# Splitting the weights of the routing's early expert projections, and four more of them in the routing

## The chip, the core and the metric

The kernel runs on one core of one Trainium2 chip. The metric is the device time of one execution in microseconds, the median of the runs shown; less is better. TensorE does the matmuls, ScalarE (ACT) and VectorE (DVE) the elementwise work, GpSimd (POOL) elementwise work in SBUF, and SyncE (SP) issues the DMAs.

## The reference, cut to what matters

Two transformer blocks run over 256 tokens of width 1024. The first ends in a product-key expert layer, and the change lies there:

```python
def chunk_fn(xc):
    q = (xc @ w_query).reshape(C, PEER_HEADS, 2, PEER_HALF)
    sc = jnp.einsum('thpd,hpnd->thpn', q, sub_keys)
    top_s, top_i = lax.top_k(sc, PEER_TOPK)
    cand_s = (top_s[:, :, 0, :, None] + top_s[:, :, 1, None, :]).reshape(...)
    best_s, best_pos = lax.top_k(cand_s, PEER_TOPK)
    gates = jax.nn.softmax(best_s, axis=-1)
    u = expert_down[experts]
    vv = expert_up[experts]
    act = jax.nn.gelu(jnp.einsum('cd,chkd->chk', xc, u), approximate=False)
    return jnp.einsum('chk,chkd->cd', gates * act, vv)
```

## The kernel before

All 16,384 experts are computed for all tokens and weighted with a mostly empty matrix of gates. They are cut into 128 chunks of 128 experts. Each chunk needs a projection (eight k-steps of a 128x128 block of `expert_down` against the 256 tokens), a Gelu, a multiplication with the gates and a product with `expert_up`.

Four stages follow each other, and a block of all engines ends each of the first three.

1. `route_phase`. Sixteen rounds make the query projections and key scores. TensorE's matmuls feed VectorE, which finds the top 16 of each (`top16`). VectorE then works alone: for eight heads it adds two lists into `cand` (L1545) and searches them, and it then forms the index of each chosen expert in four rounds of `match` (L1568), `picked` (L1571) and a reduction (L1575). Meanwhile TensorE does the projections of the first `EARLY` = 24 chunks (`Ahead.project`, L1300), as plain float32 matmuls on the loaded weights `raw`, and ScalarE the Gelus (L1311). The gates' exponential (L1514) stands behind the Gelu of chunk `BEFORE_GATE` - 1. At the end TensorE waits for VectorE's indices and gates and turns them (L1489). SP loads a half chunk as soon as TensorE has read the half that lies in its buffer (L1292).
2. `spread_phase` builds the matrix of gates from one-hot products, 32 groups of eight tokens, and between them TensorE does `LATE` = 20 more plain projections. `early` holds the first `READY` = `EARLY` + `LATE` chunks, already multiplied with their gates; `spread` holds the gates of the others.
3. `experts_phase`. For the first `READY` chunks TensorE only adds (12 matmuls of 512 columns, `add`). For the others it does `both`: the projection of the next chunk in three passes (`Projections`), and the addition.
4. The second block of the reference.

A projection in three passes has both operands split into a float32r part and the rest. ScalarE copies the weight to `high`, another engine subtracts it from the raw weight to give `low`, and TensorE makes `high`x`high`, `high`x`low` and `low`x`high` (L230, L231, L232). The query projections of the routing are split in this way already, in buffers `w_high` and `w_low`: ScalarE at L1499, GpSimd at L1450, half a chunk (128x512) each time. In the expert stage VectorE makes `low`.

The order of each engine's work is the program's order; engines meet at semaphores. `over_chunks` writes chunks 0 and 1 out and loops over pairs behind them.

Of the kernel before, what the change touches and what calls it, by code (L numbers as in the profile page):

```python
# [22 lines left out]
F32 = mybir.dt.float32  # L23
# [3 lines left out]
ALU = mybir.AluOpType  # L27
ACT = mybir.ActivationFunctionType
# [3 lines left out]
SEQ = 256  # L32
NT = SEQ // P
D = 1024
KD = D // P
# [6 lines left out]
HEADS_P = 8  # L42
TOPK = 16
SLOTS = HEADS_P * TOPK
EARLY = 24
LATE = 20
BEFORE_GATE = 16
LEAD = 8
FINE = 8
READY = EARLY + LATE  # L50
REST = 1
# [107 lines left out]
def wait(eng, sem, value):  # L159

    if isinstance(value, int) and value <= 0:
        return
    eng.wait_ge(sem, value)
# [51 lines left out]
def second_row_high(act, hT, full, ready):  # L215

    for n in (2, 3):
        act.activation(row_window(hT[0], n), row_window(full, n), ACT.Copy).then_inc(ready, 1)
# [9 lines left out]
def three_passes(pe, out, lhs, rhs, start, stop):  # L228

    pe.matmul(out, lhs[0], rhs[0], start=start, stop=False, skip_group_check=True)  # L230
    pe.matmul(out, lhs[0], rhs[1], start=False, stop=False, skip_group_check=True)  # L231
    return pe.matmul(out, lhs[1], rhs[0], start=False, stop=stop, skip_group_check=True)  # L232
# [1081 lines left out]
class Projections:  # L1314
# [18 lines left out]
    def half(self, h):  # L1333
        return slice(KD // 2 * h, KD // 2 * (h + 1))
# [33 lines left out]
def over_chunks(eng, lo, hi, one):  # L1368

    if lo == 0:  # L1370
        one(0, 0)
        one(1, 1)
        lo = 2
    with eng.Fori(lo // 2, hi // 2) as i:
        for b in range(2):
            one(i * 2 + b, b)


def route_phase(nc, weights, hT, whole, sbt, slots, raw, landed, early, ahead):
# [3 lines left out]
    HP = 2 * HEADS_P  # L1383
    NW = len(raw)
    with ExitStack() as c:  # L1385
        def sb(n, s, dt=F32):
            return c.enter_context(nc.sbuf_tensor(f"route_{n}", s, dt))
# [4 lines left out]
        def sem(n):  # L1392
            return c.enter_context(nc.semaphore(f"route_{n}"))
# [11 lines left out]
        shifted = sb("shifted", [P, NT, SLOTS])  # L1405
        gate = sb("gate", [P, NT, SLOTS])
# [8 lines left out]
        w_high, w_low = [[sb(f"{n}{b}", [P, KD, P], F32R) for b in range(2)] for n in ("w_high", "w_low")]  # L1415
        q_ready, q_kept, s_ready, s_kept, w_highs, w_lows = [sem(n) for n in ("q", "q_kept", "s", "s_kept", "w_highs", "w_lows")]
        shifted_ready, gate_exp, cols_ready = [sem(n) for n in ("shifted", "gate_exp", "cols")]
        row_high, row_low = sem("row_high"), sem("row_low")
        block = c.enter_context(nc.Block())

        def steps(eng, one):
            rounds = HP // NW
            for b in range(NW):
                one(b, b, 0)
            with eng.Fori(1, rounds - 1) as i:
                for b in range(NW):
                    one(i * NW + b, b, i)
            for b in range(NW):
                one((rounds - 1) * NW + b, b, rounds - 1)

        @block.sync
        def _(sp):

            for b in range(2):
                ahead.load(sp, b, b)
            with sp.Fori(0, HP // NW - 1) as i:
                for b in range(NW):
                    sp.wait_ge(s_ready, i * NW + b + 1)
                    sp.dma_start(raw[b][:], weights[i * NW + b + NW]).then_inc(landed[b], 16)
            over_chunks(sp, 2, EARLY + 2, lambda n, b: ahead.load(sp, n, b))  # L1440

        @block.gpsimd
        def _(pool):
            def weight_low(hp, b, i):
                if isinstance(hp, int) and hp < 2:
                    return
                for h in range(2):
                    k = slice(KD // 2 * h, KD // 2 * (h + 1))
                    pool.wait_ge(w_highs, hp * 2 + (h - 3))
                    pool.tensor_tensor(w_low[b % 2][:, k], raw[b][:, k], w_high[b % 2][:, k].bitcast(F32),  # L1450
                                       ALU.subtract).then_inc(w_lows, 1)
            steps(pool, weight_low)

        @block.tensor
        def _(pe):
            def one(hp, b, i):
                wait(pe, q_kept, hp - 1)
                first = isinstance(hp, int) and hp < 2
                if isinstance(hp, int) and hp == 2:
                    pe.wait_ge(row_low, 2)  # L1460
                for k in range(KD):
                    if first:
                        mm = pe.matmul(ahead.u[b][:, P:SEQ], raw[b][:, k, :], ahead.h[:, k, P:SEQ], start=k == 0, stop=k == KD - 1,
                                       skip_group_check=True)
                        continue
                    if k % (KD // 2) == 0:
                        pe.wait_ge(w_lows, hp * 2 + (k // (KD // 2) - 3))
                    mm = three_passes(pe, qp[b % 2][:, 0:SEQ], [v[b % 2][:, k, :] for v in (w_high, w_low)],
                                      [v[:, k, :] for v in hT], k == 0, k == KD - 1)
                mm.then_inc(q_ready, 1)  # L1470
                if not isinstance(hp, int) or hp > 0:
                    scores_of(hp - 1, (b - 1) % NW)

            def scores_of(hp, b):
                pe.wait_ge(q_kept, hp + 1)
                if isinstance(hp, int) and hp < 2:
                    pe.wait_ge(landed[b], 16)
                wait(pe, s_kept, hp - 1)
                for t in range(NT):
                    mm = pe.matmul(sp_[b % 2][:, t * P:(t + 1) * P], qh[b % 2][:, t * P:(t + 1) * P], raw[b][:, KD, :],  # L1480
                                   start=True, stop=True)
                mm.then_inc(s_ready, 1)
            steps(pe, one)
            scores_of(HP - 1, NW - 1)
            over_chunks(pe, 0, EARLY, lambda n, b: ahead.project(pe, n, b))
            for n, src in enumerate((index[1], coarse, fine, gate)):
                pe.wait_ge(cols_ready, n + 1)
                for t in range(NT):
                    pe.transpose(slots[:, n, t * P:(t + 1) * P], src[:, t, :], sbt["ident"][:])  # L1489

        @block.scalar
        def _(act):
            def weight_high(hp, b, i):
                act.wait_ge(landed[b], i * 16 + 16)
                if not isinstance(hp, int) or hp > 3:
                    wait(act, q_ready, hp - 1)
                for h in range(2):
                    k = slice(KD // 2 * h, KD // 2 * (h + 1))
                    act.activation(w_high[b % 2][:, k], raw[b][:, k], ACT.Copy).then_inc(w_highs, 1)  # L1499

            def one(hp, b, i):
                if not isinstance(hp, int) or 2 <= hp + 1 < HP:
                    weight_high(hp + 1, (b + 1) % NW, i + (b + 1) // NW)
                act.wait_ge(q_ready, hp + 1)
                wait(act, s_ready, hp - 1)
                steps_in = ahead.u[b] if isinstance(hp, int) and hp < 2 else qp[b % 2]
                act.activation(qh[b % 2][:], steps_in[:, 0:SEQ], ACT.Copy).then_inc(q_kept, 1)
            second_row_high(act, hT, whole, row_high)
            steps(act, one)
            def early_chunk(n, b):  # L1510
                ahead.gelu(act, n, b, early[:, n, :])
            over_chunks(act, 0, BEFORE_GATE, early_chunk)
            act.wait_ge(shifted_ready, 1)
            act.activation(gate[:], shifted[:], ACT.Exp).then_inc(gate_exp, 1)  # L1514
            over_chunks(act, BEFORE_GATE, EARLY, early_chunk)

        @block.vector
        def _(dve):
# [80 lines left out]
def spread_phase(nc, slots, iota, early, spread, ahead, load_first):  # L1599
# [15 lines left out]
    def merged_rows(g):  # L1615

        return EARLY + sum(j <= g for j in joins)

    with ExitStack() as c:
# [13 lines left out]
        @block.sync  # L1633
        def _(sp):
            for n in range(EARLY + 2, READY):
                ahead.load(sp, n, n % 2)
            sp.wait_ge(ahead.projected, READY * 2)
            load_first(sp)
# [437 lines left out]
```

## Time and profile before

| | |
|---|---|
| median of 3 runs | 1578.44 us (1575.54 to 1579.21) |
| profiled execution | 1575.72 us, its span 1573.9 us |
| busy: TensorE, VectorE, ScalarE, GpSimd | 98%, 64%, 44%, 3% of the span |
| projections in the routing | 234.5 to 317.5 us |
| spread stage | 318 to 448 us |
| expert stage | 449 to 1044 us |

A share of busy time says how full an engine is, not how much of its work could go. The time of the profiled execution is 1.8 us above its span; sums are made against it.

### The profile page before, as it was taken

The page shows a single profiled execution, that of the slowest core. Times are in us where ns is not written, and L with a number is a line of the kernel's source. Part 1 is how long each engine was busy: PE and PEld are TensorE (multiplying, and loading weights), DVE is VectorE, ACT ScalarE, POOL GpSimd, SP SyncE. Part 2 cuts the span into 40 slices and gives each one's busy share as a digit, 9 for nine tenths or more (in the row PEclk, how much of TensorE's full clock was granted, in tenths as well). Part 3 has the DMA queues.
Part 4 walks back from the last instruction along what each step waited for, and adds up shares of the span by engine and source line. Part 5 has one row for each costly group of instructions (what it writes and reads, how often), then busy time and mean ns, then how long its engine had stood idle before and what let it go on. Part 6 is the DMA issues. An engine that isn't in the chain of part 4 may idle for free. (4 is left out here: it accounts for less than half of the span.)

```text
span 1573.9 us, 29022 instructions
## 1 busy us (share of the span) xinstructions
PE 1535.9 (98%) x8999; PEld 1339.9 (85%) x8999; DVE 1008.4 (64%) x2440; ACT 692.3 (44%) x1478; POOL 41.9 (3%) x42
## 2 busy tenths in 40 slices
PE   7998999999999999999999999999999999999998
PEld 4665798889978889999999999979999999759994
DVE  4666589978877766666666666665555555247762
ACT  2443241222234444444444444446666666326651
POOL 0000260000000000000000000000000000000000
PEclk9999999999999999999999999999999999999999
DMA  7420244422245555555555555557544444317630
GB/s 289 160 101 1 70 139 148 153 94 86 82 160 188 196 189 188 186 187 186 187 187 187 187 186 187 186 172 228 176 148 148 147 147 147 94 39 224 172 101 27
DMA packets 163511, 239.30 MB, mean 152 GB/s; under 512 B 41712, under 2 KB 91376, under 8 KB 161904
## 3 DMA queue, kind: packets, MB, share of 16 engines
q1 hardware_dynamic: 163440, 238.42, 46.6%
q8 instruction: 37, 0.61, 0.1%
q14 instruction: 34, 0.28, 0.1%
HBM read 237.09 MB, written 1.29 MB: 151 GB/s over the span
## 5 line engine op out<-in xcount | busy, mean ns | idle before, releaser
L230 PE MATMUL experts_acc<-experts_uh,experts_wh 128*128 128x512 f32 x512 | 200.6, 392 | 1.6 <-DVE experts_ul L1838 1.6
L231 PE MATMUL experts_acc<-experts_ul,experts_wh 128*128 128x512 f32 x512 | 200.2, 391 | 0.0
L232 PE MATMUL experts_acc<-experts_uh,experts_wl 128*128 128x512 f32 x512 | 199.2, 389 | 0.0
L232 PE MATMUL projection<-hT_high,down_low 128*128 128x256 f32 x672 | 190.2, 283 | 0.0
L231 PE MATMUL projection<-hT_low,down_high 128*128 128x256 f32 x672 | 190.1, 283 | 0.0
L230 PE MATMUL projection<-hT_high,down_high 128*128 128x256 f32 x672 | 189.7, 282 | 0.0
L1808 ACT ACTIVATE experts_uh<-whole 128x512 fp32r<-128x512 f32 x256 | 146.8, 624 | 67.2 <-PE experts_acc L232 60.9
L1838 DVE TENSOR_TENSOR experts_ul<-whole,experts_uh 128x512 fp32r<-128x512 f32 x256 | 164.8, 685 | 1.9 <-ACT experts_uh L1808 1.9
L1300 PE MATMUL plain_u<-whole,down_raw 128*128 128x256 f32 x704 | 157.3, 379 | 0.4 <-PEq L1385 0.4
L1300 PEld LDWEIGHTS plain_u<-whole,down_raw 128*128 128x128 f32 x704 | 131.3, 190 | 17.2 <-issue 0.7
L1844 DVE TENSOR_TENSOR experts_full<-experts_full,spread 128x256 f32<-128x256 f32 x84 | 35.8, 426 | 158.1 <-ACT experts_full L1365 158.1
L231 PEld LDWEIGHTS projection<-hT_low,down_high 128*128 128x128 f32 x672 | 128.7, 191 | 3.2
L230 PEld LDWEIGHTS projection<-hT_high,down_high 128*128 128x128 f32 x672 | 128.7, 191 | 3.2
L230 PE MATMUL mix_a_pj<-mix_a_wh,hT_high 128*128 128x384 f32 x368 | 129.1, 351 | 0.0
L232 PEld LDWEIGHTS projection<-hT_high,down_low 128*128 128x128 f32 x672 | 128.7, 191 | 0.0
L1341 ACT ACTIVATE down_high<-down_raw 128x512 fp32r<-128x512 f32 x168 | 105.2, 632 | 43.5 <-DMA down_raw<-in_downT 42.8
L232 PE MATMUL mix_a_pj<-mix_a_wh,hT_low 128*128 128x384 f32 x368 | 123.5, 336 | 0.0
L231 PE MATMUL mix_a_pj<-mix_a_wl,hT_high 128*128 128x384 f32 x368 | 123.5, 336 | 0.0
L1365 ACT ACTIVATE experts_full<-projection 128x256 f32<-128x256 f32 x84 | 32.3, 384 | 205.5 <-PE projection L232 205.5
L232 PEld LDWEIGHTS experts_acc<-experts_uh,experts_wl 128*128 128x128 f32 x512 | 96.2, 188 | 20.7
L230 PEld LDWEIGHTS experts_acc<-experts_uh,experts_wh 128*128 128x128 f32 x512 | 96.5, 188 | 20.3 <-DVE experts_ul L1838 1.0
L231 PEld LDWEIGHTS experts_acc<-experts_ul,experts_wh 128*128 128x128 f32 x512 | 96.5, 188 | 16.7
(392 smaller groups left out, 3001.5 us busy)
## 6 DMA issues: line engine op xcount, KB each, us to landing
down_raw<-in_downT SPq DMA_DIRECT2D x256, 256.0 KB, 3.5
whole<-in_up SPq DMA_DIRECT2D x256, 256.0 KB, 2.8
mix_raw<-in_wa SPq DMA_DIRECT2D x46, 768.0 KB, 6.1
block_w_raw<-in_w SPq DMA_DIRECT2D x16, 768.0 KB, 6.1
mix_raw<-in_wb SPq DMA_DIRECT2D x16, 768.0 KB, 6.7
route_raw<-in_route SPq DMA_DIRECT2D x16, 576.0 KB, 3.8
wo<-in_wo SPq DMA_DIRECT2D x4, 1024.0 KB, 8.2
mix_a_w_gate<-in_wa SPq DMA_DIRECT2D x8, 512.0 KB, 7.3
```

The source lines that it names most:

```text
L230: pe.matmul(out, lhs[0], rhs[0], start=start, stop=False, skip_group_check=True)
L231: pe.matmul(out, lhs[0], rhs[1], start=False, stop=False, skip_group_check=True)
L232: return pe.matmul(out, lhs[1], rhs[0], start=False, stop=stop, skip_group_check=True)
L1300: mm = pe.matmul(self.u[b][:, 0:SEQ], self.raw[b][:, k, :], self.h[:, k, :], start=k == 0, stop=k == KD - 1, skip_group_check=True)
L1341: act.activation(self.high[b][:, self.half(h)], self.raw[b][:, self.half(h)], ACT.Copy).then_inc(self.highs, 1)
L1365: act.activation(into, self.u[b][:, 0:SEQ], ACT.Gelu).then_inc(self.done, 1)
L1808: act.activation(uh[b][:, w], raw_u[b][:, w], ACT.Copy).then_inc(u_high, 1)
L1838: dve.tensor_tensor(ul[b][:, w], raw_u[b][:, w], uh[b][:, w].bitcast(F32), ALU.subtract).then_inc(u_low, 1)
L1844: dve.tensor_tensor(full[:], full[:], spread[:, n - READY, :], ALU.mult)
```

## The change

`EARLY` goes from 24 to 28, so `READY` goes from 44 to 48, and `BEFORE_GATE` from 16 to 22. Chunks 0 and 1 stay plain. Chunks 2 to 27 of the routing are projected in three passes: ScalarE makes `w_high`, GpSimd `w_low`, TensorE 24 matmuls in place of 8. SP reloads a raw half when GpSimd has subtracted from it, where before it waited for TensorE. ScalarE makes the `high` of chunk n+1 before the Gelu of chunk n. The buffers `w_high` and `w_low` are those of the query projections.

```diff
@@ -42,9 +42,10 @@
 HEADS_P = 8
 TOPK = 16
 SLOTS = HEADS_P * TOPK
-EARLY = 24
+EARLY = 28
+SPLIT = 28
 LATE = 20
-BEFORE_GATE = 16
+BEFORE_GATE = 22
 LEAD = 8
 FINE = 8
 READY = EARLY + LATE
@@ -1418,6 +1419,15 @@
         row_high, row_low = sem("row_high"), sem("row_low")
         block = c.enter_context(nc.Block())
 
+        QUERY_HALVES = (HP - 2) * 2
+
+        def halves_split(n, h):
+
+            return QUERY_HALVES + (n - 2) * 2 + h + 1
+
+        def half(h):
+            return slice(KD // 2 * h, KD // 2 * (h + 1))
+
         def steps(eng, one):
             rounds = HP // NW
             for b in range(NW):
@@ -1437,7 +1447,16 @@
                 for b in range(NW):
                     sp.wait_ge(s_ready, i * NW + b + 1)
                     sp.dma_start(raw[b][:], weights[i * NW + b + NW]).then_inc(landed[b], 16)
-            over_chunks(sp, 2, EARLY + 2, lambda n, b: ahead.load(sp, n, b))
+
+            def load_split(n, b):
+                for h in range(2):
+                    sp.wait_ge(w_lows, halves_split(n - 2, h))
+                    sp.dma_start(ahead.raw[b][:, half(h)], ahead.down[n][:, half(h)]).then_inc(ahead.landed[b][h], 16)
+            for b in range(2):
+                ahead.load(sp, 2 + b, b)
+            over_chunks(sp, 4, SPLIT + 2, load_split)
+            if SPLIT < EARLY:
+                over_chunks(sp, SPLIT + 2, EARLY + 2, lambda n, b: ahead.load(sp, n, b))
 
         @block.gpsimd
         def _(pool):
@@ -1450,6 +1469,13 @@
                     pool.tensor_tensor(w_low[b % 2][:, k], raw[b][:, k], w_high[b % 2][:, k].bitcast(F32),
                                        ALU.subtract).then_inc(w_lows, 1)
             steps(pool, weight_low)
+
+            def down_low(n, b):
+                for h in range(2):
+                    pool.wait_ge(w_highs, halves_split(n, h))
+                    pool.tensor_tensor(w_low[b][:, half(h)], ahead.raw[b][:, half(h)], w_high[b][:, half(h)].bitcast(F32),
+                                       ALU.subtract).then_inc(w_lows, 1)
+            over_chunks(pool, 2, SPLIT, down_low)
 
         @block.tensor
         def _(pe):
@@ -1482,7 +1508,21 @@
                 mm.then_inc(s_ready, 1)
             steps(pe, one)
             scores_of(HP - 1, NW - 1)
-            over_chunks(pe, 0, EARLY, lambda n, b: ahead.project(pe, n, b))
+
+            def project_split(n, b):
+                for h in range(2):
+                    pe.wait_ge(w_lows, halves_split(n, h))
+                    if h == 0:
+                        pe.wait_ge(ahead.done, n - 1)
+                    for k in range(KD // 2 * h, KD // 2 * (h + 1)):
+                        mm = three_passes(pe, ahead.u[b][:, 0:SEQ], [v[b][:, k, :] for v in (w_high, w_low)],
+                                          [v[:, k, :] for v in hT], k == 0, k == KD - 1)
+                    mm.then_inc(ahead.projected, 1)
+            for b in range(2):
+                ahead.project(pe, b, b)
+            over_chunks(pe, 2, SPLIT, project_split)
+            if SPLIT < EARLY:
+                over_chunks(pe, SPLIT, EARLY, lambda n, b: ahead.project(pe, n, b))
             for n, src in enumerate((index[1], coarse, fine, gate)):
                 pe.wait_ge(cols_ready, n + 1)
                 for t in range(NT):
@@ -1507,12 +1547,36 @@
                 act.activation(qh[b % 2][:], steps_in[:, 0:SEQ], ACT.Copy).then_inc(q_kept, 1)
             second_row_high(act, hT, whole, row_high)
             steps(act, one)
-            def early_chunk(n, b):
+
+            def down_high(n, b):
+                for h in range(2):
+                    act.wait_ge(ahead.landed[b][h], (n - b) * 8 + 16)
+                    act.wait_ge(ahead.projected, n * 2 + (h - 3))
+                    act.activation(w_high[b][:, half(h)], ahead.raw[b][:, half(h)], ACT.Copy).then_inc(w_highs, 1)
+
+            def plain_chunk(n, b):
                 ahead.gelu(act, n, b, early[:, n, :])
-            over_chunks(act, 0, BEFORE_GATE, early_chunk)
-            act.wait_ge(shifted_ready, 1)
-            act.activation(gate[:], shifted[:], ACT.Exp).then_inc(gate_exp, 1)
-            over_chunks(act, BEFORE_GATE, EARLY, early_chunk)
+
+            def split_chunk(n, b):
+                down_high(n + 1, 1 - b)
+                plain_chunk(n, b)
+
+            def gates():
+                act.wait_ge(shifted_ready, 1)
+                act.activation(gate[:], shifted[:], ACT.Exp).then_inc(gate_exp, 1)
+            plain_chunk(0, 0)
+            split_chunk(1, 1)
+            first = min(BEFORE_GATE, SPLIT - 2)
+            over_chunks(act, 2, first, split_chunk)
+            if BEFORE_GATE < SPLIT:
+                gates()
+                over_chunks(act, first, SPLIT - 2, split_chunk)
+            split_chunk(SPLIT - 2, 0)
+            plain_chunk(SPLIT - 1, 1)
+            if BEFORE_GATE > SPLIT:
+                over_chunks(act, SPLIT, BEFORE_GATE, plain_chunk)
+                gates()
+                over_chunks(act, BEFORE_GATE, EARLY, plain_chunk)
 
         @block.vector
         def _(dve):
```

## Rows read from the trace of the kernel before

**Rows 1.** The page: busy time by engine, granted TensorE clock in 40 slices.

```profile
PE 1535.9 (98%) x8999; PEld 1339.9 (85%) x8999; DVE 1008.4 (64%) x2440; ACT 692.3 (44%) x1478; POOL 41.9 (3%) x42
...
PEclk9999999999999999999999999999999999999999
```

**Rows 2.** Busy time by stretch: length, PE, PEld, DVE, ACT, POOL, clock, DMA.

```profile
290.00:318.00 28.00, 28.00 (x134) 24.67 (x133) 24.31 (x21) 10.23 (x15) 0.00 (x0) 1.00 0.47 152
330.00:446.00 116.00, 115.76 (x763) 106.94 (x762) 94.85 (x128) 31.93 (x97) 0.00 (x0) 1.00 0.24 78
```

**Rows 3.** ScalarE in order of time, projections of the routing.

```profile
238.16 0.38 ACT L1311 ACTIVATE early<-plain_u 128x256 f32<-128x256 f32 x1 [2.96 <-PE plain_u L1300]
...
290.45 1.28 ACT L1514 ACT_TABLE_LOAD   x1
...
300.48 1.28 ACT L1311 ACT_TABLE_LOAD   x1 [3.14 <-PE plain_u L1300]
...
317.68 0.38 ACT L1311 ACTIVATE early<-plain_u 128x256 f32 x1 [1.72 <-PE plain_u L1300]
```

**Rows 4.** All engines in order of time, where the routing ends.

```profile
315.12 0.49 DVE L1595 TENSOR_TENSOR route_gate<-route_gate,route_ginv 128x128 f32<-128x128 f32 x2
...
317.39 0.38 PE L1489 MATMUL slots<-ident,route_index 128*128 128x128 f32 x2
```

**Rows 5.** TensorE in order of time, one round of the routing.

```profile
193.75 0.36 PE L230 MATMUL route_qp<-hT_high,route_w_high 128*128 128x256 f32 x1
...
196.71 0.61 PE L1480 MATMUL route_sp<-route_raw,route_qh 128*128 128x128 f32 x4
197.07 0.36 PE L230 MATMUL route_qp<-hT_high,route_w_high 128*128 128x256 f32 x1
```

**Rows 6.** Tiles projection and experts_acc: ns min/median/max, first and last start.

```profile
L230 PE MATMUL projection<-hT_high,down_high x672: 277/283/283, 571.2 to 1037.4; 128*128 128x256 f32 x168
...
L230 PE MATMUL experts_acc<-experts_uh,experts_wh x512: 389/389/504, 450.4 to 1043.2; 128*128 128x512 f32 x171
...
L232 PE MATMUL experts_acc<-experts_uh,experts_wl x512: 387/389/397, 451.0 to 1043.6; 128*128 128x512 f32 x171
```

**Rows 7.** GpSimd in order of time: its first pieces and a late round.

```profile
185.73 5.00 POOL L1450 TENSOR_TENSOR route_w_low<-route_raw,route_w_high 128x512 fp32r<-128x512 f32 x4 [169.28 <-ACT route_w_high L1499]
...
228.96 2.53 POOL L1450 TENSOR_TENSOR route_w_low<-route_raw,route_w_high 128x512 fp32r<-128x512 f32 x2 [1.32 <-ACT route_w_high L1499]
```

**Rows 8.** VectorE in order of time, four places of the routing.

```profile
183.34 1.30 DVE L225 TENSOR_TENSOR hT_low<-whole,hT_high 128x512 fp32r<-128x512 f32 x2 [1.39 <-ACT hT_high L218]
...
240.46 0.75 DVE L1545 TENSOR_TENSOR route_cand<-route_topv 128x256 f32<-128x256 f32 x2
...
282.34 0.49 DVE L1555 TENSOR_TENSOR route_shifted<-route_bestv 128x128 f32<-128x128 f32 x2
...
283.65 2.29 DVE L1568 TENSOR_TENSOR route_match<-route_partf,iota 128x2048 f32<-128x2048 f32 x1
```

**Rows 9.** VectorE's groups by shape, 240.4 to 317 us.

```profile
L1571 DVE TENSOR_TENSOR route_picked<-route_match,route_topi 128x2048 f32<-128x2048 f32 x4 | 9.2, 2292 | 0.3
...
L1575 DVE TENSOR_REDUCE route_index<-route_picked 128x128 f32<-128x2048 f32 x4 | 9.1, 2286 | 0.3
...
L1545 DVE TENSOR_TENSOR route_cand<-route_topv 128x256 f32<-128x256 f32 x16 | 6.1, 422 | 0.5
```

**Rows 10.** Tiles route_w_low and route_rest: ns min/median/max, first and last start.

```profile
L1450 POOL TENSOR_TENSOR route_w_low<-route_raw,route_w_high x28: 1266/1286/1297, 185.7 to 230.2; 128x512 fp32r<-128x512 f32 x28
...
L1526 DVE MAX8 route_topv<-route_rest x32: 276/286/297, 188.8 to 239.1; 128x8 f32<-128x128 f32 x32
```

**Rows 11.** ScalarE's groups by shape, 180 to 460 us.

```profile
L1499 ACT ACTIVATE route_w_high<-route_raw 128x512 fp32r<-128x512 f32 x28 | 16.2, 625 | 7.7 <-DMA route_raw<-in_route 7.7
```

**Rows 12.** Tile down_raw, 234 to 318 us: from issue to landing.

```profile
DMA to landing us min/median/max: 2.5/2.7/3.0
```

**Rows 13.** VectorE's groups, 318 to 449 us.

```profile
L1670 DVE TENSOR_TENSOR early<-early,spread_g 128x208 f32<-128x208 f32 (+20 forms) x32 | 14.0, 436 | 21.6 <-ACT spread L1722 21.6
```

## The prediction, made before the change was run

> **What bounds the kernel now.** I read the page first: TensorE is busy 98% of the span, at the full clock (2.4 GHz) in every slice [rows 1]. Then the table by stretch, for the end of the routing and the spread stage: TensorE is busy throughout, and VectorE nearly so [rows 2]. Then the order of time where the routing ends. TensorE sets it, but only just: VectorE's last gate operation ends at 315.6 (315.12 + 0.49), and TensorE starts to turn its results at 317.39, as soon as the last projection is through [rows 4]. So VectorE's chain of top-16 searches and index arithmetic has 1.8 us of slack; whatever takes more than that from the projections' time only uncovers it. Last, I looked for who else works there: GpSimd does nothing behind 231.5 (its last piece starts at 228.96), and its pieces before that are the same subtraction that the change adds [rows 7].
>
> **The terms on TensorE.** A plain projection: the Gelus follow each other from 238.16 to 317.68, 23 intervals, 3.457 us each [rows 3]; 24 take 83.0. A projection in three passes: in the routing its 24 matmuls and the step to the scores take 2.96 us (193.75 to 196.71) [rows 5]. In the expert stage 44 additions alone take 450.4 to 571.2, 2.745 each, and 84 of projection and addition 571.2 to 1043.6, 5.624 each, which leaves 2.88 for the projection [rows 6]. I take 2.88.
>
> - Expert stage: four chunks fewer need a projection there: 4 x 2.88 = -11.5 us. Their Gelus, splits and loads go too, but they lie beside TensorE. This term I hold for sure.
> - Routing: 2 x 3.457 + 26 x 2.88 = 81.8 in place of 83.0, -1.2 us, if TensorE is never made to wait.
> - Spread stage: VectorE's merge covers four rows more, 32 elements of some 1.05 ns (2048 elements take 2.29 us and 256 take 0.42 [rows 9]) x 32 groups = 1.1 us, and it idles 21.6 us there [rows 13]. TensorE is busy 115.76 of 116 us [rows 2] with unchanged work. Nothing.
>
> **Supply.** A chunk needs from ScalarE two copies of 0.6 us [rows 11] and a Gelu of 0.38 [rows 3], from GpSimd two halves, 2.53 us [rows 7], of 2.88. GpSimd is thus 88% full. The loop through ScalarE, with an estimated 0.1 at each handover: end of chunk n-1, Gelu 0.38, first copy 0.6, first subtraction 1.28, three handovers: 2.6 of the 2.88 that TensorE spends on chunk n. The loop through SP: a load lands in 2.7 us [rows 12], then 0.6 + 1.28 and three handovers make 4.9 of the 5.76 that a buffer has. Both close, with little to spare. At the start, chunks 2 and 3 cannot be loaded before chunk 0 and 1 are read: about +0.5 us. The exponential of the gates now stands before the copy of chunk 23: load of its table 1.28, itself 0.42, so the loop takes 4.3 in place of 2.6 once, +1.4 us; and the Gelu's table is loaded again in the loop every second chunk behind it (300.48, as now [rows 3]), 3.9 in place of 2.6, +1.0. These 2.9 us count only if nothing slower covers them. VectorE's own use of the gates comes at 314, and the indices are ready for the exponential at 283 [rows 8], chunk 21's end is about 299: no wait for VectorE.
>
> **The unknown: GpSimd beside VectorE.** Until now GpSimd worked only beside VectorE's searches, which read one operand. Next to those neither is slowed: a subtraction takes 1266 to 1297 ns in all 28 cases, a MAX8 276 to 297 with and without GpSimd [rows 10]. But VectorE's operations on two operands in SBUF never met it: the last before GpSimd ends at 184.64 (183.34 + 1.30) and GpSimd starts at 185.73 [rows 7, 8]. Now 26 x 2.53 = 66 us of subtraction run beside 16 `cand` additions (6.1 us) and eight operations of 2.29 us (18.3 us) on two operands [rows 9]. The cost lies between nothing and full exclusion, where one waits until the other is done. Rows that lean to the upper end: GpSimd takes 1286 ns for 512 elements of two operands where ScalarE takes 625 for 512 of one [rows 10, 11], as if operands were fetched one after the other on a path that is scarce. And with GpSimd 88% full, a loss of over 12% reaches TensorE whole. I take the upper end. Its price, with each waiting its turn:
>
> - Heads, 240.46 to 282.34 [rows 8]: GpSimd is busy 88% of the time, so an addition waits 0.88 x 0.64 = 0.56 us on average, 16 of them 9 us: VectorE's index stage starts at 283.65 + 9 = 292.6. GpSimd loses 0.75 us per head, about its slack, so TensorE goes on at 2.9 per chunk from 241.9 and has done 19.5 chunks by then.
> - Four index rounds: `match` 2.29, one half subtraction 1.28, `picked` 2.29, two halves 2.53 beside the reduction of 2.29 = 8.4 us for three halves, one chunk and a half. 4 x 8.4 = 33.6 us, to 326.2, 25.5 chunks. TensorE gets a chunk per 5.6 us here and idles half the time.
> - VectorE's path is free then: 2.5 x 2.88 = 7.2, end at 333.4. If GpSimd gets both halves between `match` and `picked`, the rounds are longer and more chunks are done in them; the end is the same within 1 us, since it is a sum of turns. VectorE's chain ends near 329.
> - Two additions of 0.42 take 0.75 together [rows 8]: starts overlap. Over some 48 changes of turn I take off 1.5 us: 332.
>
> The Trainium skill speaks against this change here. "SBUF — State Buffer", section "Who interferes with whom", says that a VectorE instruction with two SBUF inputs and a GpSimd instruction that reads SBUF take one shared read port in turn, the second blocking for the whole length of the first. No row before shows it; by it the sum is the upper end, without it the first rival below.
>
> **Sum of the forecast.** Routing's projections end at 332 in place of 317.5: +14.5. Experts -11.5. Together +3.0: 1575.7 becomes 1578.7 profiled. The median stands 2.7 above the profiled execution, so 1581.4, say 1581. If a start-up part of 0.15 us (0.42 less 256 x 1.05 ns) holds no path, the end is 330 or a little less; with more lost at each turn 337: own range 1575 to 1587.
>
> **Rivals.**
>
> 1. *No contention.* For it: the unslowed rows above [rows 10]. The projections end at 234.5 + 81.8 + 2.9 = 319.2, past VectorE's 315.6: +1.7 - 11.5 = -9.8, 1568.6 us. Chance 0.33.
> 2. *VectorE is starved, slower.* If GpSimd, with its next half already queued, goes first whenever both ask, an addition waits 1.9 us in place of 0.56. The heads take 16 x 1.9 = 30 more and end near 314, GpSimd is done near 318, and the 29 us of index rounds then stand alone, to 346. From the point that VectorE's waits sum to over 16 us (332 - 315.6) it sets the end. +29 - 11.5 = +17, 1596 us. Against it: GpSimd has a gap in each round [rows 7]. Chance 0.04.
> 3. *The clock falls.* TensorE is busy 2.88 of 5.6 us in the index rounds; if the granted clock, 2.4 GHz now, goes to 1.2, a chunk costs 5.76, and the last 2.5 chunks 7.2 more, then a few us of the spread stage: 1591 us. No row before has so loose a stretch. Chance 0.03.
> 4. *Partial sharing*, between forecast and first rival, about 1575: 0.06.
>
> **Numbers.** Forecast 0.54, in which the same is 0.31, slower 0.20, faster 0.03. Within 0.3% (4.7 us) is what a measurement can't tell from no change. Faster: 0.33 + 0.03 + 0.03 of partial sharing = 0.39. Same: 0.31 + 0.03 = 0.34. Slower: 0.20 + 0.04 + 0.03 = 0.27. The range must hold the first rival and most of the forecast: 1566 to 1588. It leaves out rivals 2 and 3 and the tails, some 0.15.
>
> **What the profile after would show.** Expert stage: 48 additions at 2.745 and 80 pairs at 5.62, 11.5 us shorter, whatever the routing does. For the forecast: `match` and `picked`, or the subtractions next to them, longer than 2.29 and 1.28 us or starting late; the index rounds 8.4 us and not 7.05; TensorE with gaps that end on GpSimd's `w_low` between 290 and 326. For the first rival: durations as before, projections 2.88 apart, and one gap near the exponential. Wrong altogether would be the supply loops: a cadence of 3 us or more among the heads, where nothing large meets GpSimd, means that copy, subtraction and load do not fit in 2.88.

## The result, and the profile after

The changed kernel takes 1581.62 us (median of 8 runs, 1579.24 to 1582.23), the kernel before 1577.76 us (8 runs): a ratio of 1.0023, 95% interval 1.0014 to 1.0032. It is slower by 3.9 us. That is clear of the noise, but within the 0.3% that the prediction called no change. The profiled execution of after took 1581.96 us, near its median, and its span is 1580.0. The profiled execution of before (1575.72 us) lay 2.0 us under the median of 8. So the two spans differ by 6.1 us where the medians differ by 3.9.

The page of after (answers to [rows 1]): TensorE is busy 8 us less in a span 6 us longer, and GpSimd goes from 41.9 to 120.4 us.

```profile
PE 1527.7 (97%) x9175; PEld 1337.6 (85%) x9175; DVE 1019.8 (65%) x2428; ACT 716.6 (45%) x1522; POOL 120.4 (8%) x94
...
POOL 0000267830000000000000000000000000000000
```

The table by stretch of after (length, PE, PEld, DVE, ACT, POOL, clock, DMA share, GB/s; answers to [rows 2]):

```profile
260.00:280.00 20.00, 20.00 (x168) 19.82 (x168) 18.75 (x61) 11.00 (x21) 17.14 (x15) 1.00 0.58 184
...
290.00:300.00 10.00, 7.26 (x58) 6.80 (x57) 9.61 (x7) 4.58 (x9) 9.31 (x5) 1.00 0.43 136
300.00:310.00 10.00, 6.88 (x53) 6.48 (x54) 9.78 (x4) 6.05 (x9) 9.63 (x6) 1.00 0.34 105
310.00:320.00 10.00, 6.60 (x49) 6.11 (x48) 9.61 (x6) 5.53 (x8) 8.37 (x5) 0.86 0.33 105
320.00:330.00 10.00, 8.56 (x56) 8.36 (x56) 9.62 (x6) 4.12 (x7) 7.11 (x6) 0.80 0.37 110
```

Look for the break at 290. From 260 to 280 TensorE has no gap, while GpSimd works 17.14 of 20 us. From 290 to 320 TensorE is busy only two thirds of the time, GpSimd and VectorE over 90%: both look like the bound, and each is waiting inside its instructions.

VectorE's groups by shape, 240 to 345 us (answers to [rows 9]):

```profile
L1609 DVE TENSOR_TENSOR route_cand<-route_topv 128x256 f32<-128x256 f32 x16 | 12.5, 820 | 0.5
L1632 DVE TENSOR_TENSOR route_match<-route_partf,iota 128x2048 f32<-128x2048 f32 x4 | 12.2, 3038 | 0.3
L1635 DVE TENSOR_TENSOR route_picked<-route_match,route_topi 128x2048 f32<-128x2048 f32 x4 | 11.9, 2970 | 0.3
```

The counts are those of before; `cand` takes 820 ns in place of 422, `match` 3038 in place of 2292. A blocked instruction is not shown as idle: its wait is in its duration. In order of time (answers to [rows 8] and [rows 4]):

```profile
240.15 1.28 DVE L1605 CAST route_topi<-route_topu 128x512 f32<-128x512 uint32 x1
241.35 1.85 DVE L1609 TENSOR_TENSOR route_cand<-route_topv 128x256 f32<-128x256 f32 x2
...
292.63 3.22 DVE L1632 TENSOR_TENSOR route_match<-route_partf,iota 128x2048 f32<-128x2048 f32 x1
295.93 3.20 DVE L1635 TENSOR_TENSOR route_picked<-route_match,route_topi 128x2048 f32<-128x2048 f32 x1
299.20 2.29 DVE L1639 TENSOR_REDUCE route_index<-route_picked 128x128 f32<-128x2048 f32 x1
301.56 3.33 DVE L1632 TENSOR_TENSOR route_match<-route_partf,iota 128x2048 f32<-128x2048 f32 x1
...
328.48 1.35 DVE L1644 TENSOR_SCALAR route_eighth<-route_index 128x256 f32<-128x256 f32 x1
...
332.80 0.49 DVE L1659 TENSOR_TENSOR route_gate<-route_gate,route_ginv 128x128 f32<-128x128 f32 x2
```

`match` starts at 292.63, where the forecast had 292.6. It takes 3.22 in place of 2.29, so it waited 0.93 us for a half subtraction that had begun; the first round takes 8.93 us to the next `match`. The last gate operation ends at 333.3. GpSimd's side, in order of time (answers to [rows 7]; the third line is one of the six of the second, by itself):

```profile
285.30 5.13 POOL L1476 TENSOR_TENSOR route_w_low<-down_raw,route_w_high 128x512 fp32r<-128x512 f32 x4 [0.67 <-ACT route_w_high L1555]
291.12 11.62 POOL L1476 TENSOR_TENSOR route_w_low<-down_raw,route_w_high 128x512 fp32r<-128x512 f32 x6 [0.68 <-ACT route_w_high L1555]
296.94 3.31 POOL L1476 TENSOR_TENSOR route_w_low<-down_raw,route_w_high 128x512 fp32r<-128x512 f32 x1
```

Four halves took 5.13 us beside the searches, and six take 11.62 beside the index rounds. The one that starts at 296.94, inside `picked` (295.93 to 299.13), ends at 300.25: 1.1 us behind `picked`, so nearly all of its own 1.29 us comes after it. That is one waiting for the other, and not both going on more slowly. TensorE's waits, 230 to 345 us (total, times, longest):

```profile
PE plain_u L231 <- POOL route_w_low L1476: 11.5, 8, 2.1
```

11.5 us, all on GpSimd's `w_low`. The first turning of indices, at 317.39 before [rows 4], is at 333.10 in after: +15.7. The first addition of the expert stage moves by the same 15.7, so the spread stage costs what it did. The tiles of the expert stage (answers to [rows 6]):

```profile
L231 PE MATMUL experts_acc<-experts_uh,experts_wh x512: 389/389/628, 466.1 to 1050.2; 128*128 128x512 f32 x171
...
L231 PE MATMUL projection<-hT_high,down_high x640: 277/283/284, 600.6 to 1044.3; 128*128 128x256 f32 x160
```

The last product (L233) starts at 1050.6. The stage took 584.5 us in place of 593.2, so 8.7 less and not 11.5; more on this below. Behind it the profiled execution of after is 0.9 us shorter than that of before, which had a granted clock of 0.91 from 1420 to 1440 us. That may be why; the change does not touch that stretch. 15.7 - 8.7 - 0.9 = 6.1 us.

### The profile page after: what moved, and what is told of

Same layout as the page of the kernel before. It is cut to its first block and busy times, and to the rows that moved or that the text cites. A ratio compares the mean times of both kernels' runs of the same rounds, so it can differ in the third digit from the quotient of the medians.

```text
span 1580.0 us, 29624 instructions
## 1 busy us (share of the span) xinstructions
PE 1527.7 (97%) x9175; PEld 1337.6 (85%) x9175; DVE 1019.8 (65%) x2428; ACT 716.6 (45%) x1522; POOL 120.4 (8%) x94
## 3 DMA queue, kind: packets, MB, share of 16 engines
HBM read 237.09 MB, written 1.29 MB: 151 GB/s over the span
## 5 line engine op out<-in xcount | busy, mean ns | idle before, releaser
L233 PE MATMUL experts_acc<-experts_uh,experts_wl 128*128 128x512 f32 x512 | 199.9, 390 | 0.0
L233 PE MATMUL projection<-hT_high,down_low 128*128 128x256 f32 x640 | 181.1, 283 | 0.0
L232 PE MATMUL projection<-hT_low,down_high 128*128 128x256 f32 x640 | 181.1, 283 | 0.0
L231 PE MATMUL projection<-hT_high,down_high 128*128 128x256 f32 x640 | 180.7, 282 | 0.0
L231 PEld LDWEIGHTS projection<-hT_high,down_high 128*128 128x128 f32 x640 | 122.5, 191 | 3.1
L232 PEld LDWEIGHTS projection<-hT_low,down_high 128*128 128x128 f32 x640 | 122.5, 191 | 3.1
L233 PE MATMUL mix_a_pj<-mix_a_wh,hT_low 128*128 128x384 f32 x368 | 123.5, 336 | 0.0
L233 PEld LDWEIGHTS projection<-hT_high,down_low 128*128 128x128 f32 x640 | 122.5, 191 | 0.0
L1342 ACT ACTIVATE down_high<-down_raw 128x512 fp32r<-128x512 f32 x160 | 100.2, 632 | 40.1 <-DMA down_raw<-in_downT 39.8
L233 PEld LDWEIGHTS experts_acc<-experts_uh,experts_wl 128*128 128x128 f32 x512 | 96.5, 188 | 20.8
L1349 DVE TENSOR_TENSOR down_low<-down_raw,down_high 128x512 fp32r<-128x512 f32 x160 | 103.0, 684 | 2.6 <-ACT down_high L1342 2.6
L660 PE MATMUL block_pj<-block_w_raw,whole 128*128 128x384 f32 x256 | 91.1, 487 | 1.0 <-PEq L1181 1.0
```

The costliest lines, as they stand in the source:

```text
L660: mm = pe.matmul(dst[:, 0:3 * P], hT[:, k, chunks[i][1] * P:(chunks[i][1] + 1) * P], pieces.raw[b][:, k, :], start=k == 0, stop=k == KD - ...
L1342: act.activation(self.high[b][:, self.half(h)], self.raw[b][:, self.half(h)], ACT.Copy).then_inc(self.highs, 1)
L1349: eng.tensor_tensor(self.low[b][:, k], self.raw[b][:, k], self.high[b][:, k].bitcast(F32), ALU.subtract).then_inc(self.lows, 1)
```

## The experiments

Each kernel was timed beside the kernel before on the same chip; that took 1577.4 us for the first four below the changed kernel, 1577.8 for the last four. Line numbers in the rows are those of each kernel.

| kernel | median us | ratio to before, 95% interval |
|---|---|---|
| changed kernel | 1581.62 | 1.0023 (1.0014 to 1.0032) |
| one operand in PSUM | 1571.25 | 0.9965 (0.9952 to 0.9978) |
| no subtraction | 1564.08 | 0.9915 (0.9902 to 0.9928) |
| four more, plain | 1579.11 | 1.0013 (1.0004 to 1.0022) |
| split to 16 | 1571.05 | 0.9959 (0.9946 to 0.9972) |
| splits alone | 1588.64 | 1.0070 (1.0056 to 1.0084) |
| PSUM and late gates | 1566.43 | 0.9927 (0.9914 to 0.9941) |
| GpSimd only writes | 1566.91 | 0.9937 (0.9924 to 0.9951) |
| late gates alone | 1579.41 | 1.0017 (1.0008 to 1.0026) |

### One operand in PSUM

```diff
-            dve.tensor_copy(topi[:], topu[:])
+            topi_ps, topv_ps = [v[:].rearrange(whole_bank, t=NT, h=HP) for v in qp]
+            partf_ps, eighth_ps = [v[:, 0:NT * SLOTS].rearrange("p (t s) -> p t s", t=NT) for v in sp_]
+            dve.tensor_copy(topi_ps, topu[:])
+            dve.tensor_copy(topv_ps, topv[:])
+            dve.drain()
```

and `topv_ps` is the second operand of `cand`, `partf_ps` the first of `match`, `topi_ps` the second of `picked`. `eighth` lies in PSUM too.

> The changed kernel, with one operand of VectorE's additions and index products in PSUM: copies of topv and topi, and partf, lie in the four banks that the query projections and scores have left, and eighth lies in PSUM too. Everything else as in the changed kernel. Theory (GpSimd and a VectorE operation take turns where both need the second way to read SBUF): match and picked are back at 2.29 us and cand at 0.42, no subtraction is longer than 1.3 us, the index rounds take 7.1 us each, and the projections end near 319.5 in place of 333.3: about 13 us less than the changed kernel, 10 less than the kernel before, some 1568. Rival (any GpSimd work beside VectorE costs, or the loops of copy, subtraction and load are too slow in the index rounds): nothing changes, some 1582.

Measured: 1571.25 us, 10 less than the changed kernel. The tiles (ns min/median/max), and three of VectorE's groups by shape (busy us, mean ns):

```profile
L1637 DVE TENSOR_TENSOR route_match<-route_sp,iota x4: 2291/2292/2292, 285.5 to 308.3; 128x2048 f32<-128x2048 f32 x4
L1640 DVE TENSOR_TENSOR route_picked<-route_match,route_qp x4: 2286/2286/2287, 287.9 to 310.7; 128x2048 f32<-128x2048 f32 x4
...
L1476 POOL TENSOR_TENSOR route_w_low<-down_raw,route_w_high x52: 1267/1292/1345, 239.6 to 321.5; 128x512 fp32r<-128x512 f32 x52
...
L1614 DVE TENSOR_TENSOR route_cand<-route_topv,route_qp 128x256 f32<-128x256 f32 x16 | 6.0, 418 | 0.6
L1624 DVE TENSOR_TENSOR route_shifted<-route_bestv 128x128 f32<-128x128 f32 x2 | 1.4, 716 | 0.1
L1631 DVE TENSOR_SCALAR route_part<-route_pos 128x256 uint32<-128x256 uint32 x1 | 0.9, 904 | 0.1
```

GpSimd reads both operands from SBUF as often as in the changed kernel, and works beside the same VectorE operations, and neither waits: `match` is at 2.29 us in all four cases, `cand` at 418 ns, and the longest subtraction is 1345 ns. Apart from one more copy (`topv`, 0.68 us), only where VectorE's operands lie was changed. What still had all its operands in SBUF still waited in this same kernel: `shifted` took 716 ns in place of 288 and one `part` 904 in place of 296. That decides for the shared reading of SBUF, and against any cost of GpSimd's presence as such. But the first turning of indices is at 324.9 and not 319.5: 5 us were lost to something else. ScalarE in order of time shows it:

```profile
301.59 1.28 ACT L1566 ACT_TABLE_LOAD   x1
...
303.32 1.28 ACT L1555 ACT_TABLE_LOAD   x1
...
305.78 1.28 ACT L1312 ACT_TABLE_LOAD   x1
...
312.25 0.39 ACT L1312 ACTIVATE early<-plain_u 128x256 f32 x1 [3.76 <-PE plain_u L233]
312.67 1.28 ACT L1555 ACT_TABLE_LOAD   x1
```

The exponential brings three loads of a function table of 1.28 us in close succession, not two: one for itself, one for the *copy* that follows it (L1555), one for the Gelu. And the loop behind it holds a load before a copy (312.67) and one before a Gelu, every second chunk. Of those behind the exponential the prediction had counted the Gelu's alone. TensorE waits 4.2 us for `w_low` there, and its granted clock is 0.79 of full speed from 300 to 310 and 0.86 from 310 to 320.

### No subtraction

```diff
-                    sp.wait_ge(w_lows, halves_split(n - 2, h))
+                    sp.wait_ge(w_highs, halves_split(n - 2, h))
...
-            over_chunks(pool, 2, SPLIT, down_low)
...
-                    pe.wait_ge(w_lows, halves_split(n, h))
+                    pe.wait_ge(w_highs, halves_split(n, h))
```

> The changed kernel without GpSimd's 52 subtractions for the projections: TensorE and the loads wait for ScalarE's copy instead, and the third pass reads stale low parts, so this leaves out part of the computation. Theory (the subtraction beside VectorE is the whole cost): VectorE's chain is back at its 75 us from the first cand to the last gate, ends near 316, and TensorE ends at about 317, with the smaller loop hiding the table loads: some 1567. Rival (ScalarE's copies, the table loads and the loads from memory hold the projections up): TensorE's gaps between 290 and 330 stay in part, 1575 or more.

Measured: 1564.08 us, 3 less than expected. The turning of the indices:

```profile
L1528 PE MATMUL slots<-ident,route_index x2: 271/272/272, 317.1 to 317.2; 128*128 128x128 f32 x2
```

At 317.1 it is where the terms put it: 26 projections in three passes, supplied by the same copies and loads, end with the 24 plain ones of before. TensorE waits 1.4 us once, at the table loads. The loops of copy and load were not the trouble. The expert stage takes 582.3 us here (450.1 to 1032.4), 10.9 less than before, so the stages account for 11.2 us of the 13.3 by the medians. The rest has no cause shown; the executions of the kernel before spread over 4 us.

### Four more, plain

The kernel before with `EARLY = 28`.

> The kernel before with EARLY at 28 and nothing else: four more projections in the routing, plain ones. By the terms of the prediction: routing 4 x 3.457 = 13.8 us longer, expert stage 11.5 shorter, together +2.3: some 1580, a little under the changed kernel. Rival (the move costs something of its own in the spread or expert stage): over +4.

```profile
L1489 PE MATMUL slots<-ident,route_index x2: 273/273/273, 331.1 to 331.2; 128*128 128x128 f32 x2
```

The routing is 13.7 us longer (331.1 against 317.39), the forecast term 13.8, and the expert stage 11.1 shorter (464.2 to 1046.3, 582.1 us, against 593.2): +2.6 by these, +1.7 by the medians. The move of a chunk is worth what the terms say, and the rival (over +4) is out.

### Split to 16

The changed kernel with `SPLIT = 16`.

> The changed kernel with SPLIT at 16: chunks 2 to 15 in three passes, 16 to 27 plain, so GpSimd is done before the index rounds begin. Theory: cand additions are still slowed (VectorE some 7.5 us late, its gates end near 323), the index rounds are not (7.1 us each); TensorE ends at 234.5 + 6.9 + 14 x 2.88 + 12 x 3.457 + 0.6 = 323.8. Routing +6.5, experts -11.5: some 1573, 9 less than the changed kernel though twelve projections are dearer on TensorE. Rival (the index rounds are not where it goes): 12 x 0.58 = 7 us more than the changed kernel, 1589.

Measured: 1571.05 us. Tiles `route_cand`, `route_match` and `slots`:

```profile
L1609 DVE TENSOR_TENSOR route_cand<-route_topv x16: 410/737/1518, 241.4 to 285.0; 128x256 f32<-128x256 f32 x16
...
L1632 DVE TENSOR_TENSOR route_match<-route_partf,iota x4: 2291/2292/2293, 291.1 to 313.2; 128x2048 f32<-128x2048 f32 x4
...
L1529 PE MATMUL slots<-ident,route_index x2: 272/272/273, 325.5 to 325.6; 128*128 128x128 f32 x2
```

`cand` still meets GpSimd (up to 1518 ns), `match` does not (2292). TensorE ends near 325 with the twelve last projections plain, where 323.8 was expected. On TensorE alone these cost 7 us more than in the changed kernel, and the kernel is 10 us faster. The index rounds are where it goes. The edit takes the copies of the last twelve chunks, with their table loads, away too; the kernels without the subtraction and with late gates alone show that those are not it.

### Splits alone

The changed kernel with `EARLY = SPLIT = 24` and `BEFORE_GATE = 18`.

> The changed kernel with EARLY and SPLIT at 24 and BEFORE_GATE at 18: chunks 2 to 23 in three passes, no chunk moved into the routing. Theory (VectorE, made late by its turns, and TensorE end together in the changed kernel, so taking four projections off only uncovers VectorE): the last index round and what follows it are no longer slowed, VectorE's gates end at about 330, the routing is some 13 us longer than before, the expert stage unchanged: some 1590. Rival (terms simply add, TensorE sets the end): 4 x 2.88 = 11.5 less than 333 for the routing, 321.6, 4 us over the kernel before: 1581.

Measured: 1588.64 us, the slowest of all. TensorE's waits, 230 to 345 us:

```profile
PE plain_u L231 <- POOL route_w_low L1476: 9.5, 6, 4.9
PE slots L1529 <- DVE route_coarse L1648: 7.5, 1, 7.5
```

It is through with its 24 chunks at 318.5, and then waits 7.5 us for `coarse`, near the end of VectorE's chain, whose last gate operation ends at 328.2. The four moved chunks in the changed kernel fill this hole: they lengthen the routing by some 5 us, not by the 11.5 of their terms, and shorten the expert stage. So without them the kernel is 11 us slower than the kernel before, and with them 4; terms of TensorE do not add here.

### Late gates alone

In the changed kernel the exponential was moved behind the last copy of a weight:

```diff
-            over_chunks(act, 2, first, split_chunk)
-            if BEFORE_GATE < SPLIT:
-                gates()
-                over_chunks(act, first, SPLIT - 2, split_chunk)
-            split_chunk(SPLIT - 2, 0)
+            over_chunks(act, 2, SPLIT - 2, split_chunk)
+            down_high(SPLIT - 1, 1)
+            gates()
+            plain_chunk(SPLIT - 2, 0)
             plain_chunk(SPLIT - 1, 1)
```

> The changed kernel with the exponential moved behind the last copy of a weight, operands all in SBUF. Theory (with GpSimd and VectorE taking turns the table loads lie under those waits): VectorE's chain sets the end and needs as long as before, so at most 3 us less than the changed kernel: 1579 to 1582. Rival (the table loads are a large part of what the changed kernel lost): 6 us less or more, 1576.

Measured: 1579.41 us. By the medians that is 2 less than the changed kernel, but the two intervals overlap, and the traces put next to nothing of it in the routing: VectorE's last gate operation ends at 333.2 as there (333.3), and the first addition starts at 465.7 in place of 466.1. `match` and `picked` are slower still (3281 and 3198 ns on average). So the taking of turns covered the table loads' price but for some 0.4 us. The expert stage of this kernel (tiles as above):

```profile
L231 PE MATMUL experts_acc<-experts_uh,experts_wh x512: 389/389/497, 465.7 to 1047.3; 128*128 128x512 f32 x171
...
L231 PE MATMUL projection<-hT_high,down_high x640: 277/283/283, 597.7 to 1041.4; 128*128 128x256 f32 x160
```

Its 48 additions alone take 465.7 to 597.7, 132.0 us, where the changed kernel's took 134.5. That is where the two profiled executions differ.

### PSUM and late gates

The two edits together.

> The kernel with one operand of VectorE's work in PSUM, and the exponential of the gates moved behind the last copy of a weight (before the Gelu of chunk 26), so no activation table is loaded between two copies. Theory (what that kernel lost against 1568 is the tables: the loads for the exponential, for the copies behind it and for the Gelus in the loop stand in the loop of copy, subtraction and product, and the gaps also lower TensorE's clock): the projections end near 317 in place of 324.8, TensorE has no gap over 1 us, the clock stays at 2.4 GHz: some 1564. Rival (the loads from memory or VectorE's stay behind it): 1569 or more.

Measured: 1566.43 us, the best of the kernels that compute everything: 0.9927 of the kernel before. Its waits, and the table by stretch from 300 to 320 us:

```profile
PE plain_u L231 <- POOL route_w_low L1476: 1.2, 2, 0.9
...
300.00:310.00 10.00, 10.00 (x85) 9.93 (x85) 9.61 (x6) 5.50 (x11) 8.76 (x7) 1.00 0.55 175
310.00:320.00 10.00, 10.00 (x86) 9.93 (x85) 9.38 (x11) 7.14 (x12) 7.64 (x6) 1.00 0.58 187
```

TensorE is busy 20 of 20 us at the full clock where the changed kernel had 13.5 of 20. The indices are turned at 320.2 us where 317 was expected; 1.6 us of the difference is that the projections begin at 236.0 in this execution and not at 234.4. Against the kernel with PSUM alone, the placement of the exponential is worth some 5 us by the medians (4.7 by the first addition, 453.2 in place of 457.9), where the changed kernel gained 0.4 in the routing: what a load costs depends on what covers it.

### GpSimd only writes

```diff
-                    pool.tensor_tensor(w_low[b][:, half(h)], ahead.raw[b][:, half(h)], w_high[b][:, half(h)].bitcast(F32),
-                                       ALU.subtract).then_inc(w_lows, 1)
-            over_chunks(pool, 2, SPLIT, down_low)
+                    pool.memset(w_low[b][:, half(h)].bitcast(F32), 0.0).then_inc(w_lows, 1)
+            for n in range(2, SPLIT):
+                down_low(n, n % 2)
```

> The changed kernel with GpSimd's 52 subtractions replaced by 52 memsets of the same half buffers (128x512, some 0.53 us): the low parts are zero, which leaves out that part of the projections. GpSimd's loop over the chunks is written out. It reads nothing, at the same places in the chain. Theory (what is shared is the second way to read): match and picked stay at 2.29 us, cand at 0.42, though casts and tensor_scalars from SBUF to SBUF may still be late; the routing ends as without the subtraction, some 1565. Rival (any GpSimd instruction keeps VectorE's two-operand work out): match and picked get longer by up to 0.53 us wherever a memset runs, the memsets are stretched to up to 2.3 us, and the end is later by some 5 us, 1570.

Measured: 1566.91 us.

```profile
L1476 POOL MEMSET route_w_low<- x52: 520/526/657, 239.7 to 314.9; 128x512 f32 x52
...
L1632 DVE TENSOR_TENSOR route_match<-route_partf,iota x4: 2291/2292/2293, 283.6 to 306.1; 128x2048 f32<-128x2048 f32 x4
```

`match` is not touched (2293 ns at most), though memsets fall into it. The memsets are 526 ns in the median and 657 at most. It is the reading that is shared, for two-operand work. GpSimd's share of the time is smaller here (52 x 0.53 = 27 us in place of 66), so the time of this kernel alone would not decide; the durations of `match` do. A tensor_scalar from SBUF to SBUF is another matter: one `part` took 700 ns in place of 296 here, with a memset beside it.

## Why the prediction was right

It was right in the sum (+3.0 forecast, +3.9 measured by the medians) and in its main mechanism, with misses in single terms that partly cancel. That the median (1581.62) falls within 1 us of the forecast (1581.4) is in part luck: the profiled execution came out at 1582.0 where 1578.7 was forecast, and the 2.7 us that the forecast put between a profiled execution and the median were nothing in after.

- *A projection in three passes costs 2.88 us on TensorE.* Right: in after, 80 pairs of projection and addition take 600.6 to 1050.6, 5.625 each, and without the subtraction 26 projections end at the time forecast.
- *GpSimd and VectorE's two-operand work take turns.* Shown, by the kernel that changes only where the operand lies. The Trainium skill ("SBUF — State Buffer", section "Who interferes with whom") states this for two SBUF inputs against a GpSimd instruction that reads SBUF, and that one that only writes does not contend with them; durations of 2292 ns with an operand in PSUM and beside memsets agree.
- *Heads, 9 us late.* The time was right (292.63), its make-up was not. The additions cost 12.5 - 6.1 = 6.4 us, not 9. The rest comes from work that the prediction had left out: the cast `topi` took 1.28 us in place of 0.43, the cast `partf` 1.31 in place of 0.29, `shifted` 1.10 in place of 0.49.
- *Index rounds of 8.4 us.* 292.63 to 328.40, 35.8 us for four with a tensor_scalar and a cast in them, where 33.6 were forecast and 29.1 had been needed (from 283.65 in [rows 8] to 312.7). The forecast let VectorE wait 1.28 us before `picked` in each round and 0.24 behind the reduction, 6.1 in all. In fact six of the eight two-operand operations waited 0.9 to 1.0 us each, 5.7 in all, and the tensor_scalar 1.0; GpSimd gets nearly four halves into a round, not three, because its half has begun when VectorE asks. The small operations between the rounds, 1.6 us in the kernel before (29.1 less 4 x 6.87), had been left out.
- *End of the projections at 332, VectorE's chain near 329.* 333.1 and 333.3. VectorE's end was forecast 4 us too early: the rounds end 2.2 us later, and the two tensor_scalars of `eighth` take 2.57 us in place of 0.59. So both engines set the end and not TensorE alone, which the kernel with splits alone confirms.
- *The table loads count only if nothing covers them.* Right in kind (some 0.4 us where the turns cover them, some 5 where nothing does), too small in size: 2.4 us had been put on them and the copies' own loads were missed. In after they stand here, ScalarE in order of time (answers to [rows 3]):

```profile
305.36 1.28 ACT L1566 ACT_TABLE_LOAD   x1
...
307.09 1.28 ACT L1555 ACT_TABLE_LOAD   x1
308.39 1.15 ACT L1555 ACTIVATE route_w_high<-down_raw 128x512 fp32r<-128x512 f32 x2
311.13 1.28 ACT L1312 ACT_TABLE_LOAD   x1 [1.59 <-PE plain_u L233]
...
314.40 1.28 ACT L1555 ACT_TABLE_LOAD   x1
...
322.15 1.28 ACT L1312 ACT_TABLE_LOAD   x1 [5.30 <-PE plain_u L233]
```

- *Expert stage -11.5 us.* The prediction held this term for sure. In the profiled execution it is -8.7, while the late gates alone have 582.0 us, -11.2. The difference is in the first additions: the 48 take 134.5 us in place of 132.0. The granted clock is 0.91 of full speed from 466 to 476 and 0.92 from 476 to 486, behind a wait of 1.8 us for VectorE's `experts_ul` that ends at 473.67. The kernel with four more plain chunks has a clock of 0.83 from 460 to 470, and yet its 48 additions take 132.1 (464.2 to 596.3). The eight spans of after go from 1577.3 to 1580.4, which this may explain; only one of them has a trace. What decides it was not tried.
- *Rival "the clock falls".* It came true for a few microseconds. The table by stretch of after, columns as above:

```profile
316.00:318.00 2.00, 1.76 (x12) 1.47 (x12) 1.93 (x1) 0.85 (x2) 2.00 (x1) 0.82 0.37 123
318.00:320.00 2.00, 0.89 (x4) 0.89 (x5) 2.00 (x1) 0.00 (x0) 2.00 (x2) 0.50 0.02 8
320.00:322.00 2.00, 2.00 (x11) 2.00 (x11) 1.93 (x2) 0.00 (x0) 1.53 (x2) 0.50 0.63 163
322.00:324.00 2.00, 2.00 (x12) 2.00 (x11) 1.92 (x2) 1.84 (x3) 0.00 (x0) 0.50 0.64 222
```

TensorE had been busy 0.08 of the 2 us from 314, and half of 318 to 320; then matmuls run at 1.2 GHz until 324, 11 or 12 of them in 2 us in place of 19. The prediction had given this 10 us. GpSimd and VectorE are busy or waiting for each other in this stretch, and the end is 1.1 us behind the forecast, so it can have cost little; no run separates it.
- *First rival, no contention, chance 0.33.* Refuted by the durations. *VectorE is starved*: its waits did not grow beyond one half at a time (1.1 us at most, `cand` at 1.51). *Partial sharing*: in the turns a blocked subtraction has nearly its whole 1.29 us still to do when VectorE is through.

## What to carry to other kernels

Before giving GpSimd elementwise work, list what VectorE does at that time by the number of SBUF operands, and by whether it is a cast or tensor_scalar from SBUF to SBUF; rows next to one-operand searches prove nothing about the rest. If the two must meet, try one operand of VectorE's work in a free PSUM bank; here it took the conflict away for the price of one small copy (0.68 us). And when a stage ends with two engines within 2 us of each other, do not add an edit's terms on one of them: the four moved chunks cost 1.7 us in the kernel before and save 7.0 in the changed one.

## What the runs showed of the hardware that had not been expected

- One-operand VectorE instructions waited too, if they were casts or tensor_scalars from SBUF to SBUF: in after `eighth` took 1.35 us in place of 0.29, the cast `topi` 1.28 in place of 0.43. The means of MAX8, the searches and the reduction did not change by 10 ns. The same page of the Trainium skill names copies, casts and tensor_scalars in a two-port mode as contending. The trace agrees as to which instructions waited; in which mode they ran it does not show.
- A blocked instruction of either engine shows the wait as busy time: 3038 ns for `match`, up to 3312 ns for a subtraction of 1.29 us. Busy shares of over 90% for both engines hid that GpSimd worked two thirds of the time (6 x 1.28 of 11.62 us) and VectorE three quarters (6.87 of 8.93).
- The first copy of a weight behind the exponential had a table load of its own (1.28 us, at 307.09), and so had the same copy of the loop when it came round again, although a Gelu stood before it (314.40). The loop's other copies, and all before the exponential, had none.
